# Three transformer blocks on one core: the embedding gate's steps kept in the product's PSUM bank, and products that take the banks in turn

## The reference, cut to what matters

```python
for i in range(2):
    h = h + mix                                   # attention, its output product
    h = h + conv_ffn(rms_norm(h, ffn_norm[i]), ...)
    gate = sigmoid(rms_norm(h, ple_norm[i]) @ ple_w_gate[i])
    h = h + (p[i] @ ple_w_proj[i]) * gate         # the embedding's step
return rms_norm(h, final_norm)
```

## Time and profile before

| | |
|---|---|
| median of 3 runs | 2036.15 us (2034.93 to 2037.29) |
| the profiled execution, its own time | 2032.93 us |
| its span, first to last instruction | 2031.1 us |
| mean granted clock of TensorE | 0.992 |
| busy: TensorE / VectorE / ScalarE / GpSimd | 1974.3 / 1199.5 / 897.1 / 1119.9 us |
| moved by DMA | 182.75 MB, 90 GB/s in the mean |

### The profile page before, as it was taken

One profiled execution on the slowest core, in us unless ns is written; L12 is line 12 of the kernel. 1 busy time (PEld: TensorE's weight loads), 2 busy tenths in 40 slices (PEclk: granted clock), 3 DMA queues, 4 the chain that ended last, 5 costly groups with the idle time before them and its releaser, 6 DMA issues.

```text
span 2031.1 us, 25621 instructions
## 1 busy us (share of the span) xinstructions
PE 1974.3 (97%) x9452; PEld 1620.5 (80%) x9452; DVE 1199.5 (59%) x1985; ACT 897.1 (44%) x1692; POOL 1119.9 (55%) x850
## 2 busy tenths in 40 slices
PE   7999999999999999999999999998999999999997
PEld 6887887878888876777788888886887888888886
DVE  6663324343333478878676646756567676646856
ACT  5544336433343455554353433434466453433442
POOL 5345544444444465464566656655774566665662
PEclk9999999999999999999999999998999999999998
DMA  4112233222232321111323222322110322222321
GB/s 156 53 68 97 93 111 125 94 99 98 104 107 95 125 73 53 52 53 63 125 94 104 93 94 94 104 98 80 68 53 32 115 93 98 100 94 94 104 94 52
DMA packets 52108, 182.75 MB, mean 90 GB/s; under 512 B 5776, under 2 KB 6160, under 8 KB 51984
## 3 DMA queue, kind: packets, MB, share of 16 engines
q1 hardware_dynamic: 51984, 181.12, 25.7%
HBM read 174.80 MB, written 6.29 MB: 89 GB/s over the span
## 4 chain that ended last, share of the span: by engine, by line
PE 91%; DVE 7%; issue 1%; ACT 1%; DMA 0%; POOL 0%; DVEq 0%; SPq 0%; ACTq 0%
PE b L385 27%; PE b L387 27%; PE b L386 27%; PE b L407 2%; PE b L399 1%; PE b L419 1%; PE b L420 1%; PE b L418 1%; PE b L440 1%; DVE ra L472 1%; PE b L430 1%; DVE fa L562 1%; PE b L400 1%; DVE sm L550 1%; PE b L401 1%
## 5 line engine op out<-in xcount | busy, mean ns | idle before, releaser
L240 POOL TENSOR_TENSOR ra<-raw,ra 128x512 fp32r<-128x512 f32 x632 | 881.3, 1402 | 789.1 <-ACT ra L281 787.6
L385 PE MATMUL b<-ra 128*128 128x512 f32 x2528 | 1005.1, 398 | 33.1 <-DVE ra L472 14.5
L387 PE MATMUL b<-ra 128*128 128x512 f32 x2528 | 989.0, 391 | 0.0
L386 PE MATMUL b<-ra 128*128 128x512 f32 x2528 | 988.4, 391 | 0.0
L281 ACT ACTIVATE ra<-raw 128x512 fp32r<-128x512 f32 x632 | 391.5, 627 | 535.3 <-PE b L387 522.8
L385 PEld LDWEIGHTS b<-ra 128*128 128x128 f32 x2528 | 477.0, 189 | 140.7 <-issue 20.9
L387 PEld LDWEIGHTS b<-ra 128*128 128x128 f32 x2528 | 476.5, 189 | 101.2
L386 PEld LDWEIGHTS b<-ra 128*128 128x128 f32 x2528 | 477.5, 189 | 93.1
L593 DVE TENSOR_TENSOR ra<-b,ra 128x512 fp32r<-128x512 f32 (+4 forms) x166 | 92.2, 568 | 56.7 <-ACT ra L326 37.0
L709 DVE TENSOR_TENSOR h<-b,h 128x512 f32<-128x512 f32 x136 | 91.7, 683 | 55.0 <-PE b L387 54.3
L326 ACT ACTIVATE ra<-b 128x512 fp32r<-128x512 f32 (+3 forms) x142 | 67.6, 485 | 111.1 <-PE b L407 110.6
(11 more groups left out here) (274 smaller groups left out, 1918.2 us busy)
## 6 DMA issues: line engine op xcount, KB each, us to landing
raw<-in_f_g SPq DMA_DIRECT2D x40, 512.0 KB, 3.5
raw<-in_f_v SPq DMA_DIRECT2D x40, 512.0 KB, 3.5
raw<-in_f_d SPq DMA_DIRECT2D x40, 512.0 KB, 3.4
raw<-in_w_up SPq DMA_DIRECT2D x32, 512.0 KB, 3.5
raw<-in_w_down SPq DMA_DIRECT2D x32, 512.0 KB, 3.5
raw<-in_p_g SPq DMA_DIRECT2D x16, 512.0 KB, 3.5
raw<-in_w_gp SPq DMA_DIRECT2D x8, 512.0 KB, 3.5
raw<-in_w_ga SPq DMA_DIRECT2D x8, 512.0 KB, 3.4
```

What stands on the lines that cost most here:

```text
L240: e.tensor_tensor(wl, src, wh.bitcast(F), ALU.subtract).then_inc(*w_low.mark(n))
L385: e.matmul(ps, wh[:, c:c + 128], xh, start=start, stop=False)
L386: e.matmul(ps, wh[:, c:c + 128], xl, start=False, stop=False)
L387: last = e.matmul(ps, wl[:, c:c + 128], xh, start=False, stop=stop)
```

## The change

The gate's chain stays in the product's bank. `scaled_out` writes back to the bank, sigmoid, `times` and `residual` work there, and `input_in_bank` (which is `parts` of `post_norm`, moved out and given arguments) makes the next input from the bank and copies it to `h`; the bank becomes free after that. In layer 1 the square is taken from the bank, and ScalarE writes `h` already multiplied by the last gain, so that `final` is a plain product of two operands. s_first takes the next four banks of LB7 in place of 0 to 3, and part d of the output products takes LB7's present order, then bank 7, in place of 0 to 7.

```diff
         elif kind == "residual":
-            hk, src, y_done, h_done = a
+            dst, src, hk, y_done, h_done = a
...
-            e.tensor_tensor(hk, src, hk, ALU.add).then_inc(*evac.mark(n))
+            e.tensor_tensor(dst, src, hk, ALU.add).then_inc(*evac.mark(n))
...
-            e.scalar_tensor_tensor(out=m.h[:, k, :], in0=m.h[:, k, :], scalar=m.vc("final", k),
-                                   in1=banks[STB][:, :], op0=ALU.mult, op1=ALU.mult).then_inc(*els.mark(n))
+            e.tensor_tensor(m.h[:, k, :], m.h[:, k, :], banks[STB][:, :], ALU.mult).then_inc(*els.mark(n))
...
+    def input_in_bank(x, k, gain, free, b, made):
+        uh, ul = x["slots"][k]
+        ps, g = banks[b][:, :], vc(gain[0], gain[1] + k)
+        yield 0, "ac", lambda: (made,)
+        done("ac", "high", row("input_high", uh, ps, g, (made,), free))
+        h_tok[k] = (done("ac", "act", row("copy_out", h[:, k, :], b, made, ())),)
+        launch(square(x, h[:, k, :], h_tok[k][0]))
+        yield 0, "v", lambda: h_tok[k]
+        n = row("input_low", (uh, ul), ps, g, h_tok[k][0], (made,), free)
+        x["tok"][k] = (done("ve", "low_v", n),)
+        bank_free[b] = (x["tok"][k][0], h_tok[k][0])
+
+    def residual_in_bank(b, j, made):
+        return done("ve", "evac", row("residual", banks[b][:, :], banks[b][:, :], h[:, j, :], (made,), h_tok[j]))
...
         yield from linear_pairs(name + "d", lambda k: part(6 + k) if ready(6 + k) else None, 8, evac,
-                                [0, 1, 2, 3, 4, 5, 6, STB])
+                                [*LB7, STB])
...
         def evac_pg(j, b, tok):
             def process():
-                i, z, v = yield from scaled(pn, b, tok, 2)
+                z = banks[b][:, :]
+                yield 0, "v", lambda: (tok, pn["rb"]) if pn["rb"] else None
+                v = done("ve", "evac", row("scaled_out", z, b, pn["rb"], (), tok))
+                stat["rb_use"] = (v,)
                 yield 0, "ac", lambda: (v,)
                 s = done("ac", "act", row("sigmoid", z, None, v))
                 yield 0, "v", lambda: (s, pl[j])
-                v = done("ve", "elem_v", row("times", z, y_chunk(j), s, pl[j]))
-                v = done("ve", "evac", row("residual", h[:, j, :], z, (v,), h_tok[j]))
-                T.release(i, v)
-                h_tok[j] = (v,)
+                v = residual_in_bank(b, j, done("ve", "elem_v", row("times", z, y_chunk(j), s, pl[j])))
                 if nxt_gain is None:
-                    launch(square(nx, h[:, j, :], v))
+                    def scale(_):
+                        h_tok[j] = bank_free[b] = (done("ac", "high", row("input_high", h[:, j, :], z, vc("final", j), (v,),
+                                                                          ())),)
+                    yield from square(nx, z, v, scale)
                 else:
-                    input_of(nx, j, nxt_gain, ub_free)
+                    yield from input_in_bank(nx, j, nxt_gain, ub_free, b, v)
             launch(process())
...
-        yield from linear("s_first", 4, 8, rhs_u, 4, lambda j, b, t: evac_first[j](0, b, t), [0, 1, 2, 3])
+        yield from linear("s_first", 4, 8, rhs_u, 4, lambda j, b, t: evac_first[j](0, b, t), LB7)
```

More of the change, by code:

```diff
@@ L1177, in add @@
         def add(j, b, tok):
-            h_tok[j] = bank_free[b] = (done("ve", "evac", row("residual", h[:, j, :], banks[b][:, :], (tok,), h_tok[j])),)
+            h_tok[j] = bank_free[b] = (done("ve", "evac", row("residual", h[:, j, :], banks[b][:, :], h[:, j, :], (tok,),
+                                                             h_tok[j])),)
         if early:
@@ L1684, in post_norm @@
             u = norm(U_A, rank=-2 if nxt[0] == "attn" else -3)
[L1686 to L1696, removed]
             def residual(k):
@@ L1704, in residual @@
                 bank_free[b] = None
-                launch(parts(k, b, v))
+                launch(input_in_bank(u, k, nxt, u_free, b, v))
                 if k + 1 < NC:
@@ L1793, in f @@
         def f(j, b, tok):
-            v = done("ve", "evac", row("residual", h[:, j, :], banks[b][:, :], (tok,), h_tok[j]))
+            v = done("ve", "evac", row("residual", h[:, j, :], banks[b][:, :], h[:, j, :], (tok,), h_tok[j]))
             h_tok[j] = bank_free[b] = (v,)
@@ L1930, in add_h @@
         def add_h(j, bk, tok):
-            h_tok[j] = bank_free[bk] = (done("ve", "evac", row("residual", h[:, j, :], banks[bk][:, :], (tok,), h_tok[j])),)
+            h_tok[j] = bank_free[bk] = (done("ve", "evac", row("residual", h[:, j, :], banks[bk][:, :], h[:, j, :], (tok,),
+                                                              h_tok[j])),)
         def down(b):
```

## The result

The changed kernel takes **2019.45 us** (median of 4 runs, 2016.23 to 2021.76) against 2036.35 us (median of 4) for the kernel before beside it: a ratio of 0.9918, 95% interval 0.9906 to 0.9931.

A forecast was written before the change was run, and what follows sets the result against it. The prediction took TensorE as the bound, so only its waits count. Its terms, 8.0 + 2.7 - 1.2 + 1.84 - 1.2 + 1.7 + 0.2, summed to 12.0 us off the 2036.15 us median: 2024.1 us, range 2021.0 to 2027 (0.70).

The forecast's parts named there:

- s_first no longer waits: Between gate product p_g and s_first: with LB7's next four banks TensorE's wait for L600 goes, 8.0 us gained.
- Slow matmuls: At s_first's start: 13 matmuls at the lower clock behind the old wait become full speed, 2.7 us gained.
- The columns' wait: Norm's column sums (L430) inside s_first: TensorE waits 0 us for the last sum, bounds 0 and 4.5.
- the first rival: Column sums in s_first: chain no quicker in the bank, L430 waits 4.5 us; 2028.6 to 2031.4 us, chance 0.08.
- The new wait in front of s_q: s_q's first product waits for bank 6, freed by L618 of s_first's third tile: 1.2 us lost.
- The first FFN behind d_o: FFN after d_o no longer waits for tile 6's addition in its banks: 1.84 us gained.
- d_o's own first tile: First tile of d_o's last part waits for bank 3, held by the product before: 1.2 us lost.
- the second FFN: FFN after s_o finds its banks free in time: 1.7 us gained.
- The end: Eight last products lose their gain column: 0.2 us gained, 0.5 at most, none if stores set the end.
- the stall only moves: Rival at s_first: one tile's `input_low` comes late, so s_first starts as late as now; 2034.9 us, chance 0.05.
- the held banks make it slower: Rival at the gate: banks held for the whole chain, over 6.3 us a tile, delay s_first; 2045.8 us, chance 0.05.
- A longer wait behind s_first: Rival before s_q: wait for L618 of 3.1 us plus clock loss, as in the other attention; 2028.8 us, chance 0.12.

The follow-up runs named there:

- the lists alone: Kernel before with only the new bank lists for s_first and the outputs' last part, chain of steps still in SBUF: 2023.47 us, ratio 0.9944.
- the fourth experiment: Changed kernel with s_q's first products in banks 1 and 0 instead of 6, 0, 1: 2021.54 us, ratio 0.9932.
- order-only kernel: Kernel before with only the sliding attention's order changed, planner's TensorE clock set 2 us on ahead of s_q: 2032.97 us, ratio 0.9993.
- the sixth, e6: Changed kernel with s_q in banks 1 and 0 and planner's TensorE clock set 2 us on ahead of s_q's fifth tile: 2022.94 us, ratio 0.9939.
- chain: Changed kernel with the two old bank lists back, steps still in the bank: 2033.45 us, ratio 0.9986.
- e8: Changed kernel with two lists of output products turned (first attention's last part, both third parts): 2017.03 us, ratio 0.9907.
- again: The changed kernel measured a second time, nothing altered: 2019.74 us, ratio 0.9926.

## Why the prediction was right where it was, and where it failed

Its terms against the traces (before less after, from the table and the timelines):

- *s_first no longer waits*, forecast 8.0: **8.1**, by the mechanism named, since the lists alone give it. The four banks were free in time, but with half the margin worked out: tile 4's L472 ended at 1401.39, 3.9 us before s_first's start where I had put 8, so the tiles followed each other at 3.9 us and not 3.0. *Slow matmuls*, 2.7: **2.8** (26.42 against 23.64 in the fourth experiment, which has neither these nor the wait in front of s_q), clock 1.00 behind p_g's end. In the order-only kernel the same wait left only 1.7 of it, so the size is that of one trace.
- *The columns' wait*, 0: **0**. L430 stands after four steps of s_first at 1416.16 (I had said three; four is what the order shows) and the last sum ended at 1412.03, 6.75 us behind s_first's start where I had put 6.3. The runs show what this zero rests on: without the bank it is 6.5 us, 3.0 of them the wait, so the first rival was the right one to fear. The rule of the page "VectorE: DVE Perf Modes" in the Trainium skill (section "Rules for kernel authors"), copy first if many steps follow, pointed the wrong way here: the kernel with the chain in SBUF is the slower by those 6.5 us.
- *The new wait in front of s_q*, 1.2: **0.9** (24.52 against 23.64 without it; 0.72 shown as idle time).
- *The first FFN behind d_o*, 1.84: **1.70**; *d_o's own first tile*, 1.2: **0.95**; *the second FFN*, 1.7: **1.69**.
- *The end*, 0.2: **0.2**. The eight products are 0.5 us shorter, 4.87 for 5.36, but from their start to the end of the span it is 8.23 us where it was 8.43 (8.42 in the two other kernels with the old end, 8.23 or 8.24 in all with the new one): what follows them takes back more than half of it, as the bound "none if the stores set the end" allowed. Most of the rest of the 1.0 us between the two traces is the length of the last column sums, 1.17 us here; it was 1.87, 1.18 and 1.81 us in the kernels with the old end and anything from 1.05 to 1.87 in those with the new one.

```profile
2006.02 1.17 PE L430 MATMUL b<-ones,tmp 128*128 128x1 f32 x8 [2.72 <-ACT tmp L357]
...
2011.74 4.87 DVE L747 TENSOR_TENSOR h<-h,b 128x512 f32<-128x512 f32 x8 [2.17 <-PE b L440]
```

**The step that failed** is the sentence "Behind the wait on TensorE stand s_q and the turns of v, and on them the first scores": it took the rest of the sliding attention as something that only shifts, and put no term for it into the sum. It was worth **2.4 us**. The order of the attention is written by a planner with a clock of its own; the change alters the durations and bank waits ahead of it, and so the order, and with it whether the last heads have products to fill TensorE's waits. Nothing in the trace of before says which way that goes: the order-only kernel took 1.7 us off the stretch of before; the fourth experiment, back in the order of before, added 3.9 to that of after (2.4 by the order, 1.5 by the clock), and the sixth, in a third order, 2.3, all with the same matmuls. A bound of 3 us down, the two waits of the last heads, and as much up would have been an honest term, and the range would have held the time.

**The range** also took a run's scatter as 1.2 us from three runs, and its lower bound does not follow from the terms named for it: 2024.1 less 1.2, 0.3 and 1.2 is 2021.4, not 2021.0. The first line of the table alone scatters by 5 us, and 19 runs of the kernel before cover 5.5. Of the 16.9 us between the medians 15.2 are the program's by the stretches of these two traces: 12.8 from the terms above (forecast 12.0; the 12.8 hold 0.1 from the stretch to the last L385), 2.4 from the attention. The rest is well within that scatter.

The rivals: *the stall only moves* and *the held banks make it slower* are out, by s_first at clock 1.00 directly behind p_g; the second would have needed over 6.3 us a tile where 3.9 were measured. *A longer wait behind s_first* is out at 0.72 us of idle time.

## What to carry to other kernels

When a wait is cut, ask of each change apart which of two things it does: here the bank lists took the wait away and gained 0.6%, and the steps in the bank, worth 0.1% alone, kept the next product's column sums from waiting in its place. Where a planner writes the order of instructions, any edit that shifts its clock is also an edit of the order far behind it; compare the two orders before pricing, and put a term with both signs in the sum. When single times scatter by more than the effect, find the stretch that scatters and compare the others: here they repeat to hundredths of a microsecond, unless TensorE's clock falls in them.

## What was not expected of the hardware

- **The scatter has a place.** Between identical programs, the time up to the 1041st matmul of L385 was 839.1 to 844.3 us, and what follows repeated to a few hundredths where the clock did. In the first trace after, 4.8 us were lost by the 49th of these matmuls (at 58.8 us, before at 54.0); the granted clock of 0 to 60 us was 0.97 there and 1.00 before, and the first column sums waited for VectorE:

```profile
26.23 1.12 PE L430 MATMUL b<-ones,ssq 128*128 128x1 f32 x8 [1.31 <-DVE ssq L478]
```

- **The clock after the same short wait differs.** The two waits of 1.30 and 1.71 us left the clock at 1.00 in one kernel and brought 1.5 us of slow matmuls in another; the last column sums, after a wait of 2.45 to 2.72 us, took between 1.05 and 1.87 us. Much of the first line's scatter is this too (chain and e8, some 4 us late at the 1041st matmul, are within 0.5 us of before at the 49th). All ten traces wait 2.4 us for the same matmul near 340 us; behind it the clock stays at 1.00 in seven and falls in three (chain, again, e8), which costs 1.4 to 1.6 us. That matmul and the 8 us from 340, before and then in the chain-only kernel:

```profile
340.43 0.47 PE L385 MATMUL b<-ra 128*128 128x512 f32 x1 [2.40 <-DVE ra L472]
...
340.00:348.00 8.00, 7.57 (x33) 6.30 (x34) 7.86 (x13) 8.00 (x17) 4.94 (x4) 1.00 0.42 154
```

```profile
340.32 0.77 PE L385 MATMUL b<-ra 128*128 128x512 f32 x1 [2.40 <-DVE ra L472]
...
340.00:348.00 8.00, 7.67 (x27) 6.28 (x28) 7.86 (x13) 8.00 (x16) 5.04 (x4) 0.79 0.42 151
```

  The waits of 3.1 us near 743 and of 2.8 to 3.0 near 812 do the same: in chain, e6 and e8 each costs some 1.4 us more than in most others. What decides it was not tried.
- **VectorE and GpSimd slow each other.** That VectorE's SBUF steps are slower beside GpSimd was in the forecast's rows only as a mean; that GpSimd pays too, 1.72 us for 1.29, was not foreseen. Where GpSimd is idle the same SBUF step takes 0.69.
